# A decoder layer on one core: attention's buffers and bias move into dead memory of the mixers, and the sample's keys are chosen in the mixers' last slots

## The chip, the cores and the metric

The kernel runs on one core of a Trainium2 chip. The metric is the device time in microseconds (us) of one execution. Engines: TensorE (PE) multiplies and transposes, VectorE (DVE) and ScalarE (ACT) do the elementwise work, GpSimd (POOL) and SyncE (SP) issue most of the DMAs. Each engine runs its own instructions in order; they meet at semaphores only.

## The reference

One inference step of one decoder layer: 1024 prompt tokens and 64 sample tokens (8 sequences of 8), model width 1024. Two parts of it bear on the change. A lightweight indexer scores every key for every query and each query keeps its 256 best admissible keys; attention then runs over those alone, with a learned bias by distance. The chunk recurrence of the retention heads is the other mixer, computed beside the projections.

```
u = rmsnorm(x);  z = u @ w_in -> qa, ka, va (attention), qi, ki, wi (indexer), qr, kr, vr, gr (retention)
score[t,s] = sum_h wi[t,h] * relu(qi[t,h] . ki[s]) * 64**-0.5        # s > t excluded
idx = top_k(score, 256)
logits = (qa . ka[idx]) * 64**-0.5 + rel_bias[bucket(pos - idx)]     # 8 heads of 64
att = softmax(logits) @ va[idx]
h = x + concat(att, silu(gr) * groupnorm(retention)) @ w_out
out = h + moe(rmsnorm(h))                                            # top-1 of 4 groups, top-2 of 8 experts
```

For a sample query the keys are 2048 past ones, read from a paged cache, and the 8 new ones of its sequence. In the kernel the sample's scores are one tile `sc_s` of 64 queries by 2112 keys (2048 past and 64 new).

## The kernel before, in words

The kernel is one program with stages one after the other, each a function with a block of code for each engine. A stage ends when all engines are through with its block; then the stage's semaphores are cleared (`stage_semaphores`), with a barrier over all engines. Tokens are worked on in 9 tiles: 8 of 128 prompt tokens and one (number 8) of 64 sample tokens. The stages that matter here, in order:

- `gate` computes the retention gate. It also makes the bias rows and writes a skewed copy of them to DRAM (`skew`), from which one load for each head gives the bias of a whole row of query blocks. The semaphore `skewed` counts these writes.
- `index_scores` writes the scores: `sc` holds those of prompt blocks 2 to 7, one behind the other, 4224 columns of f32; `sc_s` those of the sample.
- `mixers` is a list of 54 projections (units), three for each tile in two rounds, with one slot of code for each unit on each engine. In the first round (units 0 to 26) they are the retention's q, k and v, in the second (27 to 53) attention's q, k and v. The weights of column group c lie in `w[:, c]`, and PE reads the normalised tokens from `uT`. Each projection is 8 matmuls (each shown as two in the trace). In the same slots a bisection halves the bounds of every query's threshold 32 times; ACT counts for the sample and two blocks, DVE for the others. Its last step falls into unit 40. From unit 41 on, `choose` makes one prompt block's mask in each slot (6 blocks, units 41 to 46): keys above the upper bound are in, and of those between the bounds as many, in order, as are still missing. Nothing of this kind stands in slots 47 to 54. In the second round DVE also sums squares and scales the heads of q and k (L758 to L769), and POOL stores K and V (L427, L429).
- `prompt_attention` goes through 32 units: block 7 down to block 0, four pairs of heads each. For each unit PE computes the scores (L1115) and adds the mask (L1121); DVE adds the bias and takes the row's maximum for each head (L1236), ACT exponentiates (L1176), DVE scales (L1245), PE transposes (L1137), ACT copies (L1187), PE multiplies with the values (L1150), and DVE copies out (L1202). PE may overwrite a unit's scores only after both of DVE's passes of the unit before. SP loads the bias of the 8 heads at the start of this stage (L1103). On DVE one step of `choose_for_sample` stands behind each second unit from unit 8 to unit 20: seven steps on the 64 by 2112 scores, which give `mask_s`. Its last large step writes `mask_s` in another order of keys than it reads (by `rearrange`), as `sample_attention` wants them.
- `sample_attention`, the output projection, the router, the experts and the combination follow.

The buffers of prompt attention (logits, probabilities and their transposes, the bias) have memory of their own, taken after that of the mixers is given back. Which slot a step falls into is written out by hand in the unit loops.

Of the kernel before, what the change touches and what calls it, by code (L numbers as in the profile page):

```python
# [6 lines left out]
ALU = mybir.AluOpType  # L7
ACT = mybir.ActivationFunctionType
F32 = mybir.dt.float32
BF16 = mybir.dt.bfloat16  # L10
# [323 lines left out]

def mixers(nc, S, A, X):

# [19 lines left out]
    with ExitStack() as ctx:  # L356
# [43 lines left out]
        def _(sp):  # L400
# [14 lines left out]
            for half in range(2):  # L415
                sp.dma_start(S["ret_prompt"].rearrange("(pr hh) d e -> hh d pr e", hh=2)[half],
                             state[half * HD:(half + 1) * HD, :, :]).then_inc(state_stored, 16)
            sp.wait_ge(s0_stored, 16 * 2 * DB)
            sp.wait_ge(state_stored, 32)
# [235 lines left out]
        def _(dve):  # L655
# [116 lines left out]
            def choose(i):  # L772
                s = X["sc"](i)
                n = s.shape[1]
                above, band, place = junk[:, :n], junk[:, SEQ:SEQ + n], A["va"][:, 6:8, :].rearrange("p i w -> p (i w)")[:, :n]
                link(nc.vector.tensor_scalar(above, s, X["hi"][:, i:i + 1], None, ALU.is_gt, ALU.add, accum_out=found[:, i:i + 1]))
                link(nc.vector.scalar_tensor_tensor(band, s, X["lo"][:, i:i + 1], above, ALU.is_ge, ALU.subtract))
                link(nc.vector.tensor_scalar(left[:, i:i + 1], found[:, i:i + 1], -1.0, float(TOPK), ALU.mult, ALU.add))
                link(nc.vector.tensor_tensor_scan(place, band, band, 0.0, ALU.add, ALU.max))
                link(nc.vector.scalar_tensor_tensor(band, place, left[:, i:i + 1], band, ALU.is_le, ALU.mult))  # L780
                link(nc.vector.scalar_tensor_tensor(X["mask"](i), band, -1.0, above, ALU.add, ALU.add))

            for u in range(UNITS + 1):
                p, c = divmod(u, 3)
# [40 lines left out]
                if 0 <= u - CHOOSE < len(blocks):  # L825
                    choose(blocks[u - CHOOSE])


# [235 lines left out]

def prompt_attention(nc, S, A, X, T, skewed):

# [7 lines left out]
    with ExitStack() as ctx:  # L1074
        sb = lambda n, s, d=F32: ctx.enter_context(nc.sbuf_tensor("a_" + n, s, d))
        sem = stage_semaphores(nc, ctx, "a_")
        logit = sb("logit", [P, 2, SEQ])
        prob = sb("prob", [P, 2, 2, SEQ])
        probT = sb("probT", [P, 2, 2, NT, P])
        peak = sb("peak", [P, 2])  # L1080
# [9 lines left out]
        block = ctx.enter_context(nc.Block())  # L1090
        bias_loaded = [sem(f"bias{pr}_loaded") for pr in range(PAIRS)]
        above, band, place = sb("above", [NS, NK], BF16), sb("band", [NS, NK], BF16), sb("place", [NS, NK])
        found, want, dve_done = sb("found", [NS, 1]), sb("want", [NS, 1]), sem("dve_done")
        half = lambda hh: slice(hh * HD, hh * HD + HD)
        keys = A["kaF"][:, :NT * W].rearrange("p (i a t) -> p i a t", i=NT, a=PAIRS)

        @block.sync
        def _(sp):
            sp.wait_ge(skewed, 16 * 2 * H)
            for h in range(H):  # L1100
                src = S["skew"][h].rearrange("p l -> (p l)")
                src = src[P - 1:P - 1 + P * (SEQ + P - 1)].rearrange("(p l) -> p l", l=SEQ + P - 1)[:, :SEQ]
                sp.dma_start(T["bias"][:, h, :], src).then_inc(bias_loaded[h // 2], 16)  # L1103

# [93 lines left out]
        def _(dve):  # L1198
# [4 lines left out]

            link = Chain(dve, dve_done)

            def choose_for_sample(step):
                s, lo, hi = X["sc_s"][:, :], X["lo"][:NS, NT:], X["hi"][:NS, NT:]
                if step == 0:
                    link(nc.vector.tensor_scalar(above[:, :], s, hi, None, ALU.is_gt, ALU.add, accum_out=found[:, :]))
                elif step == 1:  # L1210
                    link(nc.vector.tensor_scalar(want[:, :], found[:, :], -1.0, float(TOPK), ALU.mult, ALU.add))
                    link(nc.vector.scalar_tensor_tensor(band[:, :], s, lo, above[:, :], ALU.is_ge, ALU.subtract))
                elif step == 2:
                    link(nc.vector.tensor_tensor_scan(place[:, :PAST // 2], band[:, :PAST // 2], band[:, :PAST // 2], 0.0, ALU.add, ALU.max))
                elif step == 3:
                    link(nc.vector.tensor_tensor_scan(place[:, PAST // 2:], band[:, PAST // 2:], band[:, PAST // 2:],
                                                      place[:, PAST // 2 - 1:PAST // 2], ALU.add, ALU.max))
                elif step == 4:
                    link(nc.vector.scalar_tensor_tensor(band[:, :], place[:, :], want[:, :], band[:, :], ALU.is_le, ALU.mult))
                elif step == 5:  # L1220
                    link(nc.vector.scalar_tensor_tensor(X["mask_s"][:, :PAST].rearrange("q (r k) -> q k r", r=16),
                                                        band[:, :PAST].rearrange("q (k r) -> q k r", r=16), -1.0,
                                                        above[:, :PAST].rearrange("q (k r) -> q k r", r=16), ALU.add, ALU.add))
                elif step == 6:
                    link(nc.vector.scalar_tensor_tensor(X["mask_s"][:, PAST:], band[:, PAST:], -1.0, above[:, PAST:], ALU.add, ALU.add))

            for u, (i, pr) in enumerate(units):
                n, off = (i + 1) * P, SEQ - (i + 1) * P
                if u < PAIRS:
                    dve.wait_ge(bias_loaded[pr], 32)  # L1230
                for hh in range(2):
# [15 lines left out]
                if u >= 2:  # L1247
                    take_out(u - 2)
                if u >= 8 and u % 2 == 0:
                    choose_for_sample((u - 8) // 2)  # L1250
            take_out(len(units) - 2)
# [950 lines left out]
def build(nc, a, outs, c):  # L2202
# [20 lines left out]
    with ExitStack() as top:  # L2223
# [29 lines left out]
        with ExitStack() as early:  # L2253
# [8 lines left out]
            total = at[NT - 1] + NT * P  # L2262
            skewed = stage_semaphores(nc, early, "bias_")("skewed")
            sc = sb(early, "sc", [P, total])
            X["sc"] = lambda i: sc[:, at[i]:at[i] + (i + 1) * P]
            X["mask"] = lambda i: X["sc"](i).bitcast(BF16)[:, :(i + 1) * P]
            X["sc_s"] = sb(early, "sc_s", [NS, NK])
            X["lo"], X["hi"] = sb(early, "lo", [P, TILES]), sb(early, "hi", [P, TILES])

            with ExitStack() as st:  # L2270
# [39 lines left out]
                A["w"] = sb(st, "w", [P, 3, KD, W])  # L2310
                gate(nc, S, A, w_gate, gate_loaded, sc[:, :D], skewed)
                A["qiT"] = va_flat[:, :2 * TOK].rearrange("p (a t) -> p a t", a=2)
# [4 lines left out]
                index_scores(nc, S, A, X)  # L2317
                mixers(nc, S, A, X)
            with ExitStack() as st:
                T["bias"] = sb(st, "bias", [P, H, SEQ])  # L2320
                prompt_attention(nc, S, A, X, T, skewed)
            load_constants(nc, "l4_", [], [(A["qaT_s"], A["att"](NT), 1.0, 0.0), (A["kaT_s"], A["ka"](NT), 1.0, 0.0),
# [40 lines left out]
```

## Time and profile before

| | us |
|---|---|
| median of 3 runs | 1778.38 |
| lowest, highest | 1778.3, 1784.95 |
| the profiled execution's own time | 1778.77 |
| its span, first to last instruction | 1776.8 |
| mean granted clock of PE, share of full speed | 0.912 |

Busy times in the span: PE 1502.7 us, DVE 752.2, ACT 510.4, POOL 170.0. The profile is one execution. A view by stretch gives the busy time of each engine between two moments; the timeline shows instructions in order of time, alike ones merged, with the idle time before them and what ended it; a wait names the instruction that came last. PEclk is the clock that PE was granted, 1.00 for 2.4 GHz and 0.50 for 1.2 GHz. PEld is PE's weight load, which runs beside its matmuls. SPq and POOLq are queues of DMA issues.

### The profile page before, as it was taken

Reading aid. Unit: us, or ns where it says so; the run is one execution under the profiler, and the core shown is the slowest. Engines: PE = TensorE matmul, PEld = TensorE weight load, DVE = VectorE, ACT = ScalarE, POOL = GpSimd, SP = SyncE. Lnnn points to the kernel's source line nnn. Section 1 sums busy time; section 2 is a strip of 40 time slices with the busy share of each in tenths; the row PEclk is TensorE's granted clock in tenths of the full one; section 3 lists DMA queues with packets and bytes.
Section 4 is the critical chain, followed back from the end, with each engine's and each line's share of the span. In section 5 each row is a group of like instructions: output and inputs, shape, how many; then the busy total and the mean of one; then the engine's idle time right before and its main releaser. Section 6 shows DMA issues by size and latency. Waiting matters only on the chain. (4 is left out here: it accounts for less than half of the span.)

```text
span 1776.8 us, 20243 instructions
## 1 busy us (share of the span) xinstructions
PE 1502.7 (85%) x7317; PEld 776.1 (44%) x7331; DVE 752.2 (42%) x1900; ACT 510.4 (29%) x958; POOL 170.0 (10%) x226
## 2 busy tenths in 40 slices
PE   3999879999999999798758988899609999999940
PEld 2455324545544444365425655455304444444430
DVE  4002625587778785378834554122331111111105
ACT  3112422535457731365513332000001111111100
POOL 0001000000000000000032330000041000010005
PEclk7899659899999999899879999899859999999975
DMA  7722220001040000200078994683117999999738
GB/s 207 213 105 100 75 78 17 1 1 25 1 142 22 24 24 24 107 1 1 1 251 361 373 379 165 228 303 117 36 19 242 352 354 354 351 355 353 255 103 304
DMA packets 152647, 285.36 MB, mean 161 GB/s; under 512 B 36776, under 2 KB 106056, under 8 KB 144200
## 3 DMA queue, kind: packets, MB, share of 16 engines
q1 hardware_dynamic: 127600, 164.35, 28.2%
q0 software_dynamic: 21264, 106.88, 16.4%
q10 hardware_dynamic: 3696, 12.98, 1.9%
q8 instruction: 53, 0.87, 0.2%
q14 instruction: 34, 0.28, 0.0%
HBM read 243.04 MB, written 46.26 MB: 163 GB/s over the span
## 5 line engine op out<-in xcount | busy, mean ns | idle before, releaser
L443 PE MATMUL x_psZ<-w,uT 128*128 128x512 f32 (+1 forms) x864 | 385.0, 601 | 6.3 <-PEq L64 6.3
L443 PEld LDWEIGHTS x_psZ<-w,uT 128*128 128x128 f32 (+1 forms) x864 | 157.2, 186 | 205.1 <-issue 204.1
L1907 PE MATMUL e_psG<-e_wgu,e_xT 128*96 128x512 f32 x512 | 227.5, 597 | 1.4 <-DVE e_xT L1962 1.4
L1973 DVE TENSOR_TENSOR e_h<-e_gate,e_psG 96x256 f32<-96x256 f32 x32 | 13.4, 418 | 311.3 <-ACT e_gate L1940 311.3
L1907 PEld LDWEIGHTS e_psG<-e_wgu,e_xT 128*96 128x96 f32 x512 | 81.6, 164 | 122.7 <-issue 122.7
L1557 PE MATMUL o_ps<-o_w,k_mixT 128*128 128x512 f32 (+1 forms) x288 | 129.4, 604 | 6.2 <-DMA o_w<-in_w_out 6.2
L1895 PE MATMUL e_psY<-e_wd,e_hT 128*96 128x512 f32 x256 | 115.2, 593 | 1.7 <-ACT e_hT L1946 1.7
L1040 DVE TENSOR_SCALAR_CACHE_REDUCE x_junk<-sc,x_mid 128x384 bf16<-128x384 f32 (+3 forms) x128 | 109.2, 909 | 1.1
L1329 PE MATMUL s_psK<-k_identity,s_ring 128*128 128x128 f32 x512 | 78.5, 297 | 33.9 <-DMA s_ring<-in_cache_k,k_quarter_id 14.2
L1329 PEld LDWEIGHTS s_psK<-k_identity,s_ring 128*128 128x128 f32 x512 | 58.7, 149 | 63.5 <-issue 23.2
L1557 PEld LDWEIGHTS o_ps<-o_w,k_mixT 128*128 128x128 f32 (+1 forms) x288 | 52.6, 188 | 71.0 <-issue 63.4
L1432 DVE COPY s_kcT<-s_psK 128x512 f32<-128x512 f32 x64 | 44.2, 691 | 68.1 <-PE s_psK L1329 68.1
L1023 ACT ACTIVATE mask_s<-sc_s,x_nmid 64x2112 bf16<-64x2112 f32 x32 | 65.7, 2052 | 21.9 <-DVE x_nmid L1036 21.9
L1115 PE MATMUL a_psS<-kaF,k_mixT 64*128 64x512 f32 (+3 forms) x192 | 43.5, 561 | 28.5 <-DVE a_peak L1236 23.8
L1930 ACT ACTIVATE e_y<-e_psY 96x1024 f32<-96x1024 f32 x32 | 32.6, 1019 | 119.5 <-PE e_psY L1895 119.5
L1405 ACT ACTIVATE s_kcT<-s_psK 128x512 f32<-128x512 f32 x64 | 38.1, 595 | 95.7 <-PE s_psK L1329 95.7
L244 PE MATMUL gt_ps<-uT,va 128*128 128x512 f32 (+1 forms) x192 | 65.0, 502 | 0.0
L1882 PE MATMUL e_psX<-k_identity,e_xg 96*128 96x96 f32 x256 | 27.1, 250 | 42.6 <-DMA e_xg<-xn_rows,e_ids 42.6
L1895 PEld LDWEIGHTS e_psY<-e_wd,e_hT 128*96 128x96 f32 x256 | 39.3, 163 | 53.6 <-issue 51.7
L1940 ACT ACTIVATE e_gate<-e_psG 96x256 f32<-96x256 f32 x32 | 12.1, 379 | 174.3 <-PE e_psG L1907 174.3
L1023 ACT ACTIVATE mask_s<-sc,x_nmid 128x1024 bf16<-128x1024 f32 x64 | 59.8, 935 | 2.1
L1176 ACT ACTIVATE a_prob<-a_logit,a_neg 128x1024 f32<-128x1024 f32 (+7 forms) x64 | 49.4, 772 | 36.1 <-DVE a_neg L1239 36.0
(334 smaller groups left out, 1999.5 us busy)
## 6 DMA issues: line engine op xcount, KB each, us to landing
e_wgu<-in_w_gate SPq DMA_DIRECT2D x32, 1024.0 KB, 10.0
e_wgu<-in_w_up SPq DMA_DIRECT2D x32, 1024.0 KB, 13.0
e_wd<-in_w_down SPq DMA_DIRECT2D x32, 1024.0 KB, 7.7
w<-in_w_in SPq DMA_DIRECT2D x6, 2048.0 KB, 9.0
y_rows<-e_y ACTq DMA_DIRECT2D x32, 384.0 KB, 7.2
y_rows<-sc SPq DMA_DIRECT2D x16, 512.0 KB, 15.7
skew<-bias_rows SPq DMA_DIRECT2D x8, 576.0 KB
n_x<-in_x_prompt SPq DMA_DIRECT2D x8, 512.0 KB, 4.2
```

The costliest lines, as they stand in the source:

```text
L244: mm = nc.tensor.matmul(ps[q % 2][:, :width(t)], w[:, k, b * P:(b + 1) * P], A["uT"][:, k, t * P:t * P + width(t)], start=(k == 0), stop=( ...
L443: mm = nc.tensor.matmul(psZ[u % 2][:rows_of(i), :], A["uT"][:, k, cols_of(i)], w[:, c, k, :], start=(k == 0), stop=(k == KD - 1))
L1023: nc.scalar.activation(junk_act[:n, :view(i).shape[1]], view(i), ACT.Sign, bias=nmid[:n, i:i + 1], accum_out=count[:n, i:i + 1]).then_inc( ...
L1040: nc.vector.tensor_scalar(junk[:, junk_at[j]:junk_at[j + 1]], view(i), mid[:, i:i + 1], None, ALU.is_ge, ALU.add, accum_out=count[:, i:i + ...
L1115: nc.tensor.matmul(psS[hh][:, k0:k0 + n].rearrange("p (i t) -> p i t", t=P), A["att"](i)[half(hh), pr, :], keys[half(hh), k0 // P:(k0 + n) ...
L1176: nc.scalar.activation(prob[:, u % 2, hh, :n], logit[:, hh, :n], ACT.Exp, bias=neg[:, hh:hh + 1], accum_out=total[:, u % 2, hh:hh + 1]).th ...
L1329: mm = nc.tensor.transpose(psK[:, q % 2, r * P:(r + 1) * P], ring[:, slot, r, pair(pr)], A["identity"][:, :])
L1405: nc.scalar.activation(kcT[:, c % 2, pr, :], psK[:, 0, :], ACT.Copy).then_inc(k_taken[0], 1)
L1432: nc.vector.tensor_copy(kcT[:, c % 2, pr, :], psK[:, 1, :]).then_inc(k_taken[1], 1)
L1557: mm = nc.tensor.matmul(ps[:n, i % 2, half * 512:(half + 1) * 512], A["mix"](i)[:, k, :], w[:, k, half * 512:(half + 1) * 512], start=(k = ...
L1895: mm = nc.tensor.matmul(psY[:, b, c * 512:(c + 1) * 512], hT[:, b, f, :], wd[:, j % RING, f, c * 512:(c + 1) * 512], start=(f == 0), stop= ...
L1907: mm = nc.tensor.matmul(psG[:CAP, b, :], xT[:, b, k, :], wgu[:, j, k, :], start=(k == 0), stop=(k == KD - 1))
```

## The change

Attention's three large buffers become views on memory that the mixers no longer need: logits and probabilities on `uT`, transposed probabilities on `w[:, 2]`, the bias on `w[:, 0:2]`. With the bias living there, its eight loads are issued by SP in the mixers: those of heads 0 to 3 when the last projection that reads `w[:, 0]` is done, those of heads 4 to 7 when the last that reads `w[:, 1]` is. Their semaphores are now taken at the start of the layer. As there is no memory to give back between the mixers and attention, the semaphores of that scope (`early_`) are released after attention and not before it.

`choose_for_sample` moves from attention's loop to the mixers' slots 47 to 52, one step each. It has six steps, since the two pieces of the mask stand together. The band is written over the scores in f32 (it was a bf16 tile), the running count goes to the upper half of `sc`, and the last piece writes `mask_s` in the order of memory and reads its two inputs across it. For that the prompt masks are packed in the lower half of `sc`.

```diff
@@ def mixers(nc, S, A, X, T), at the end of sync
+            sp.wait_ge(T["skewed"], 16 * 2 * H)
+            for h in range(H):
+                if h % 4 == 0:
+                    sp.wait_ge(z_ready, UNITS - 2 + h // 4)
+                src = S["skew"][h].rearrange("p l -> (p l)")
+                src = src[P - 1:P - 1 + P * (SEQ + P - 1)].rearrange("(p l) -> p l", l=SEQ + P - 1)[:, :SEQ]
+                sp.dma_start(T["bias"][:, h, :], src).then_inc(T["bias_loaded"][h // 2], 16)
             sp.wait_ge(s0_stored, 16 * 2 * DB)
             sp.wait_ge(state_stored, 32)
@@ mixers, vector
+            def choose_for_sample(step):
+                s, lo, hi, c = X["sc_s"][:, :], X["lo"][:NS, NT:], X["hi"][:NS, NT:], slice(NT, NT + 1)
+                above, place = junk[:NS, :NK], X["sc_spare"][:NS, :]
+                by_row = lambda a: a[:, :PAST].rearrange("q (k r) -> q r k", r=16)
+                half = NK // 2
+                if step == 0:
+                    link(nc.vector.tensor_scalar(above, s, hi, None, ALU.is_gt, ALU.add, accum_out=found[:NS, c]))
+                elif step == 1:
+                    link(nc.vector.tensor_scalar(left[:NS, c], found[:NS, c], -1.0, float(TOPK), ALU.mult, ALU.add))
+                    link(nc.vector.scalar_tensor_tensor(s, s, lo, above, ALU.is_ge, ALU.subtract))
+                elif step == 2:
+                    link(nc.vector.tensor_tensor_scan(place[:, :half], s[:, :half], s[:, :half], 0.0, ALU.add, ALU.max))
+                elif step == 3:
+                    link(nc.vector.tensor_tensor_scan(place[:, half:], s[:, half:], s[:, half:], place[:, half - 1:half], ALU.add, ALU.max))
+                elif step == 4:
+                    link(nc.vector.scalar_tensor_tensor(s, place, left[:NS, c], s, ALU.is_le, ALU.mult))
+                elif step == 5:
+                    link(nc.vector.scalar_tensor_tensor(X["mask_s"][:, PAST:], s[:, PAST:], -1.0, above[:, PAST:], ALU.add, ALU.add))
+                    link(nc.vector.scalar_tensor_tensor(X["mask_s"][:, :PAST].rearrange("q (r k) -> q r k", r=16), by_row(s), -1.0,
+                                                        by_row(above), ALU.add, ALU.add))
@@ mixers, vector, in the loop over slots, behind choose
+                if 0 <= u - CHOOSE - len(blocks):
+                    choose_for_sample(u - CHOOSE - len(blocks))
@@ def prompt_attention
-        logit = sb("logit", [P, 2, SEQ])
-        prob = sb("prob", [P, 2, 2, SEQ])
-        probT = sb("probT", [P, 2, 2, NT, P])
+        spare = A["uT"][:, :, :].rearrange("p k t -> p (k t)")
+        logit = spare[:, :2 * SEQ].rearrange("p (a s) -> p a s", a=2)
+        prob = spare[:, 2 * SEQ:6 * SEQ].rearrange("p (j a s) -> p j a s", j=2, a=2)
+        probT = A["w"][:, 2, :, :].rearrange("p k n -> p (k n)").rearrange("p (j a b t) -> p j a b t", j=2, a=2, b=NT)
-        @block.sync
-        def _(sp):
-            sp.wait_ge(skewed, 16 * 2 * H)
...
-                if u >= 8 and u % 2 == 0:
-                    choose_for_sample((u - 8) // 2)
@@ def build
-            X["mask"] = lambda i: X["sc"](i).bitcast(BF16)[:, :(i + 1) * P]
+            X["mask"] = lambda i: sc[:, :].bitcast(BF16)[:, at[i]:at[i] + (i + 1) * P]
+            X["sc_spare"] = sc[:, total - NK:]
...
+                T["bias"] = A["w"][:, 0:2, :, :].rearrange("p c k n -> p (c k n)").rearrange("p (h s) -> p h s", h=H)
...
-            with ExitStack() as st:
-                T["bias"] = sb(st, "bias", [P, H, SEQ])
-                prompt_attention(nc, S, A, X, T, skewed)
+                prompt_attention(nc, A, X, T)
```

## Rows read from the trace of the kernel before

**Rows 1.** Busy time by stretch; (x) counts instructions, PEclk is the granted clock.

```profile
core 0: us, PE busy (x) PEld busy (x) DVE busy (x) ACT busy (x) POOL busy (x), PEclk, DMA share, GB/s
...
679.00:722.00 43.00, 42.82 (x112) 19.54 (x110) 13.45 (x24) 8.55 (x20) 2.69 (x5) 1.00 0.08 31
...
722.00:728.00 6.00, 0.88 (x6) 0.70 (x8) 0.00 (x0) 1.48 (x4) 0.54 (x1) 0.94 0.11 44
...
790.00:862.00 72.00, 53.98 (x475) 35.28 (x480) 61.48 (x139) 35.63 (x86) 0.00 (x0) 0.93 0.01 1
```

**Rows 2.** Timeline over the seam: start, duration, engine, line, operation, [idle before <-releaser].

```profile
707.49 13.90 PE L443 MATMUL x_psZ<-w,uT 128*128 128x512 f32 x32
...
722.31 0.54 POOL L429 DMA_DIRECT2D out<-va  x1 [2.98 <-ACT va L570]
...
727.71 5.45 SPq L1103 DMA_DIRECT2D bias<-skew  x8
...
731.34 0.81 PE L1121 MATMUL a_psS<-sc,k_identity_b 128*128 128x512 bf16 x3 [0.16 <-issue]
...
734.86 1.22 DVE L1236 CUSTOM_DVE_ANT_0 a_logit<-a_psS,bias 128x1024 f32<-128x1024 f32 x1 [16.36 <-DMA bias<-skew]
...
737.48 3.69 PE L1115 MATMUL a_psS<-kaF,k_mixT 64*128 64x512 f32 x8 [5.33 <-DVE a_peak L1236]
...
744.51 1.99 PE L1115 MATMUL a_psS<-kaF,k_mixT 64*128 64x512 f32 x8
```

**Rows 3.** Groups by line, attention: shapes, count, busy us, mean ns, idle before.

```profile
L1221 DVE SCALAR_TENSOR_TENSOR mask_s<-a_band,a_above 64x2048 bf16<-64x2048 bf16 x1 | 9.3, 9253 | 0.0
...
L1216 DVE TENSOR_TENSOR_SCAN a_place<-a_band,a_place 64x1088 f32<-64x1088 bf16 x1 | 2.5, 2467 | 0.0
...
L1212 DVE SCALAR_TENSOR_TENSOR a_band<-sc_s,lo,a_above 64x2112 bf16<-64x2112 f32 x1 | 2.4, 2410 | 0.0
...
L1219 DVE SCALAR_TENSOR_TENSOR a_band<-a_place,a_want,a_band 64x2112 bf16<-64x2112 f32 x1 | 2.4, 2400 | 0.0
...
L1209 DVE TENSOR_SCALAR_CACHE_REDUCE a_above<-sc_s,hi 64x2112 bf16<-64x2112 f32 x1 | 2.4, 2394 | 0.0
...
L1214 DVE TENSOR_TENSOR_SCAN a_place<-a_band 64x1024 f32<-64x1024 bf16 x1 | 2.3, 2273 | 0.0
...
L1225 DVE SCALAR_TENSOR_TENSOR mask_s<-a_band,a_above 64x64 bf16<-64x64 bf16 x1 | 0.2, 206 | 0.0
```

**Rows 4.** Waits of PE, 794 to 858 us: in total, times, longest.

```profile
PE a_psS L1115 <- DVE a_peak L1236: 17.0, 6, 9.1
```

**Rows 5.** Timeline of PE in attention, around the longest step.

```profile
844.28 1.13 PE L1115 MATMUL a_psS<-kaF,k_mixT 64*128 64x512 f32 x4
...
847.49 0.66 PE L1150 MATMUL a_psO<-a_probT,va 128*64 128x128 f32 x8
...
857.27 1.65 PE L1115 MATMUL a_psS<-kaF,k_mixT 64*128 64x384 f32 x4 [9.12 <-DVE a_peak L1236]
...
862.23 0.92 PE L1115 MATMUL a_psS<-kaF,k_mixT 64*128 64x384 f32 x4
```

**Rows 6.** Busy time by stretch, around the longest step.

```profile
845.00:857.00 12.00, 2.99 (x27) 1.86 (x26) 11.40 (x9) 1.55 (x4) 0.00 (x0) 0.72 0.00 0
```

**Rows 7.** Timeline: the last K store is issued.

```profile
718.79 0.54 POOL L427 DMA_DIRECT2D out<-x_nat  x1 [17.42 <-DVE x_nat L769]
```

**Rows 8.** DVE, single lines: duration min/median/max in ns, first and last start.

```profile
L1466 DVE COPY s_bias<-s_logit x1: 2401/2401/2401, 916.8 to 916.8; 128x2048 f32<-128x2048 f32 x1
...
L1751 DVE TENSOR_REDUCE g_el<-g_prod x1: 660/660/660, 1280.8 to 1280.8; 128x72 f32<-128x288 f32 x1
...
L1784 DVE TENSOR_REDUCE g_s<-g_prod x6: 452/453/455, 1292.2 to 1298.3; 128x9 f32<-128x288 f32 x6
```

**Rows 9.** DMA issues by line: count, KB each, median us to landing.

```profile
bias<-skew SPq DMA_DIRECT2D x8, 512.0 KB, 8.3
out<-va POOLq DMA_DIRECT2D x4, 256.0 KB, 2.5
```

More of the change, by code:

```diff
@@ L332, in _, with mixers @@
             pool.wait_ge(stored[1], 16 * (TILES // 2))
-def mixers(nc, S, A, X):
+def mixers(nc, S, A, X, T):
     order = [NT] + list(range(NT))
@@ L1058, in bisection, with prompt_attention @@
     return act_step, dve_begin, count_keys, move_bounds, junk
-def prompt_attention(nc, S, A, X, T, skewed):
+def prompt_attention(nc, A, X, T):
     units = [(i, pr) for i in reversed(range(NT)) for pr in range(PAIRS)]
@@ L1090, in prompt_attention @@
         block = ctx.enter_context(nc.Block())
-        bias_loaded = [sem(f"bias{pr}_loaded") for pr in range(PAIRS)]
-        above, band, place = sb("above", [NS, NK], BF16), sb("band", [NS, NK], BF16), sb("place", [NS, NK])
-        found, want, dve_done = sb("found", [NS, 1]), sb("want", [NS, 1]), sem("dve_done")
         half = lambda hh: slice(hh * HD, hh * HD + HD)
         keys = A["kaF"][:, :NT * W].rearrange("p (i a t) -> p i a t", i=NT, a=PAIRS)
-        @block.sync
-        def _(sp):
-            sp.wait_ge(skewed, 16 * 2 * H)
[L1100 to L1103, printed above, removed]
         @block.tensor
@@ L1202, in take_out @@
                 nc.vector.tensor_copy(A["att"](i)[:, pr, :], psO[:, u % 2, :P]).then_inc(o_taken, 1)
[L1204 to L1225, printed above, removed]
             for u, (i, pr) in enumerate(units):
@@ L1229, in _ @@
                 if u < PAIRS:
-                    dve.wait_ge(bias_loaded[pr], 32)
+                    dve.wait_ge(T["bias_loaded"][pr], 32)
                 for hh in range(2):
@@ L2262, in build @@
             total = at[NT - 1] + NT * P
-            skewed = stage_semaphores(nc, early, "bias_")("skewed")
+            of_bias = stage_semaphores(nc, early, "bias_")
+            T["skewed"], T["bias_loaded"] = of_bias("skewed"), [of_bias(f"loaded{pr}") for pr in range(PAIRS)]
             sc = sb(early, "sc", [P, total])
             X["sc"] = lambda i: sc[:, at[i]:at[i] + (i + 1) * P]
-            X["mask"] = lambda i: X["sc"](i).bitcast(BF16)[:, :(i + 1) * P]
+            X["mask"] = lambda i: sc[:, :].bitcast(BF16)[:, at[i]:at[i] + (i + 1) * P]
+            X["sc_spare"] = sc[:, total - NK:]
             X["sc_s"] = sb(early, "sc_s", [NS, NK])
@@ L2310, in build @@
                 A["w"] = sb(st, "w", [P, 3, KD, W])
-                gate(nc, S, A, w_gate, gate_loaded, sc[:, :D], skewed)
+                T["bias"] = A["w"][:, 0:2, :, :].rearrange("p c k n -> p (c k n)").rearrange("p (h s) -> p h s", h=H)
+                gate(nc, S, A, w_gate, gate_loaded, sc[:, :D], T["skewed"])
                 A["qiT"] = va_flat[:, :2 * TOK].rearrange("p (a t) -> p a t", a=2)
@@ L2317, in build @@
                 index_scores(nc, S, A, X)
-                mixers(nc, S, A, X)
-            with ExitStack() as st:
-                T["bias"] = sb(st, "bias", [P, H, SEQ])
-                prompt_attention(nc, S, A, X, T, skewed)
+                mixers(nc, S, A, X, T)
+                prompt_attention(nc, A, X, T)
             load_constants(nc, "l4_", [], [(A["qaT_s"], A["att"](NT), 1.0, 0.0), (A["kaT_s"], A["ka"](NT), 1.0, 0.0),
```

## The prediction

> **What bounds the kernel now.** I read the busy times by stretch first, since the change touches three stages and nothing else [rows 1]. At the end of the mixers (679 to 722 us) PE is busy 42.8 of 43 us at full clock and VectorE (DVE) 13.45 of 43: PE is the bound, DVE has some 29 us of room. In attention's blocks 5 to 3 (790 to 862 us) it is the other way round: PE 54.0 of 72 us, DVE 61.5. Between the two lies a seam, 722 to 728 us, in which PE has 0.9 us of work. Second, the timeline over the seam [rows 2]: the last V store is issued at 722.31, attention begins at 727.7 with eight loads of the bias, the scores of the first unit are there at 732.15 (731.34 and 0.81), but DVE adds the bias only at 734.86 and PE comes back at 737.48. Third, the groups of DVE's choose steps in attention [rows 3], and what PE waited for from 794 to 858 us: 17.0 us in 6 waits, each before the next scores, for DVE's peak [rows 4].
>
> **1. The seven choose steps leave attention (gain).** They cost 2.39, 2.41, 2.27, 2.47, 2.40, 9.25 and 0.21 us [rows 3], with a read-out and a small scalar 21.6 us of DVE time. DVE runs in order, so each sits in front of the next unit's two logit passes; PE, which needs those to free psS, waits. That is the 17.0 us in 6 waits, the longest 9.12 before 857.27 [rows 4, 5]. It is less than 21.6, since PE is a little behind DVE in units without a step and takes up part of each. With the steps gone, is DVE late next? No: of its 61.5 us [rows 1] 21.4 are these steps; 40.1 remain for what PE does in 54 us. PE becomes the bound, so the whole 17.0 us goes. There is a second part. In the long wait the granted clock falls (mean 0.72 over 845 to 857 us [rows 6]), and PE starts slow at 857.27: its next turn of scores, transposes and values lasts until 862.23, 4.96 us [rows 5]. The same round before it, begun at 844.28 with the larger scores of block 3, had its last values issued at 847.5 and ended by 848.15, 3.8 to 3.9 us; the score matmuls show the size, 1.65 us at 857.27 against 0.92 at 862.23 [rows 5]. Less 0.2 us for the smaller scores that round would take 3.6, so I take 1.4 us (bounds 0.7, from the score matmuls alone, and 1.6). Sum of part 1: 17.0 + 1.4 = 18.4 us.
>
> **2. The bias is read before the mixers end (gain).** SyncE now issues the loads of heads 0 to 3 when the last tile's first projection is done, and of heads 4 to 7 one projection later. PE does the last two projections from 707.49 to 721.4, with 0.6 us of transposes ahead of them [rows 2], so a projection is 7.0 us and the two moments are 707 and 714.4. Before, eight issues took 5.45 us of the queue and a load landed 8.3 us after its issue [rows 2, 9]; half of them would be in by 707 + 2.7 + 8.3 = 718, the others by 725.5 at that pace, and half the traffic at a time lands sooner. Attention starts at 727.7 and its first unit needs heads 0 and 1 only, so the wait is gone. What is late next is PE's first mask matmul: the logit pass can start at about 732.0 (the first head's mask is a little before 732.15) and not at 734.86. Gain 2.9 us (bounds 0 and 2.9 for the wait alone). PE then starts the second scores at 734.6 and not 737.48. Whether it starts slow, as before (3.69 us against 1.99 at 744.51 [rows 2]), is open: the idle stretch is 2.5 us and no longer 5.3. I take the same slow start; a clock that holds would give 1.7 us more.
> What is queued behind the moved loads: on SyncE only its waits for the stores of the states, issued some twenty projections earlier. The other queue is POOL's, with the last K and V stores. K is issued at 718.79, V at 722.31 and lands 2.5 us later at 724.8 [rows 2, 7, 9]; this landing ends the mixers. The second half of the bias (2.1 MB) starts at 714.4 and shares the DMA engines with the K store. The V store meets at most its tail. I take 0, bounds 0 and 2.5 us (a landing twice as long).
>
> **3. The choose steps enter the last slots of the mixers.** One step in each of slots 47 to 52: 2.5, 2.5, 2.35, 2.35, 2.4 and the last. The scans are 1056 long, between 2.27 for 1024 and 2.47 for 1088 [rows 3]; the band is f32 now, the same element count. Slots are some 7 us and DVE works 13.45 of 43 us in them [rows 1], so 14.6 us more fit, and what stands behind a step on DVE (scaling of heads, K's gain) is wanted by PE only a slot later. Cover gone would cost the step, 2.4 us each. The exception is the last, in slot 52: on DVE it stands between the last sum of squares and the scaling whose result is the K store at 718.79 [rows 7] and PE's last transpose. POOL issues in order, K and then V, 0.54 us an issue, V at 722.31. So K may be issued as late as 721.77: DVE can lose 2.98 us there. The last step is a 64-wide piece (0.21) and the 2048-wide one, which I call T: the cost to the end of the mixers is T - 2.75, if that is positive.
> T is not in the trace. It was 9.25 us for bf16 inputs in order and a bf16 output scattered at 256 bytes [rows 3]. Now the output is in order and both inputs are scattered (f32 at 64 bytes, bf16 at 32). Nearest rows: two inputs and all in order, 2.40 for 2112 [rows 3]; an f32 output scattered at 512 bytes, 2.40 for 2048 [rows 8]; an f32 input in steps of 32 bytes, 288 elements, 660 ns against 453 in order [rows 8], 0.72 ns more an element, which is 1.5 us on 2048 for one input and 3.0 for two. So T lies between 2.35 and 9.25, with 5.3 between them. The nearest rows say that what was dear was the 2-byte scattered write, since a 4-byte one was not. I take T = 2.4, cost 0; bounds 0 and 6.5 us.
> This last part is where a rule speaks against the change. The trace first: the scattered f32 write took 1.17 ns an element, the scattered bf16 write 4.5 [rows 3, 8]. The Trainium skill, "SBUF — State Buffer", section "Door 1: The DMA port swizzle", has a note by which accesses are only free while at least two of them hit the same 16-byte line; both new inputs go to another line with every element. By that rule T would stay near 9 us, the sum 6.5 us less; by the rows on f32 it would be 2.4. The f32 write at 512 bytes does not agree with the rule, the f32 read [rows 8] agrees in part.
>
> **4. Buffers.** Logits, probabilities and their transposes lie in memory that the mixers are done with; same shapes, same instructions: 0. One release of semaphores moves from before attention to behind it; both places are on the path: 0, bounds -0.5 and +0.5. Masks lie elsewhere, with the same width: 0.
>
> **Sum.** 18.4 + 2.9 = 21.3 us. The profiled execution took 1778.77 us (span 1776.8 and 2.0 around it), which makes 1757.5. It stands 0.4 above the median of the runs shown, 1778.38, so against that 1757.1. All later stages begin behind barriers and shift as one.
>
> **Rivals.**
> A. The scattered reads are as dear as the scattered write. For it: the steps of 64 and 32 bytes, and the reduction with a scattered input [rows 8]. Against: the f32 row at 512 bytes. The mixers end 6.5 us later: gain 14.8, 1763.6 us. Chance 0.15.
> B. The bias traffic holds up the last stores, or comes in no earlier than before. For it: at 8.3 us a load the last ones would land at 725.5, behind the V store. Against: only 2.1 MB are under way after 714.4. Price up to 2.5 us, or the 2.9 of part 2: about 1760. Chance 0.10.
> C. Slower than before: T by itself is so long that it eats everything. That begins where T - 2.75 is over 21.3, T over 24 us or 11.8 ns an element, 2.6 times the dearest DVE row here (4.5 ns). At 14 ns, T is 29 us and the time 1783. For it speaks only that two inputs are scattered and not one output. Chance 0.03. Milder, T of 15 to 24 us, would leave it within the band of no change: 0.03.
> D. The change does not do what it says in attention: DVE's own order of work holds PE up after all, with no step in it. DVE has 40.1 us of work for PE's 54.0 [rows 1], so it could be so only in single units where two passes and two scalings come late together; at 0.2 to 0.3 us in each of ten units it costs 2 or 3 of the 17.0 us: 1760. Chance 0.06.
>
> **How the numbers follow.** The forecast has 0.63, the rest as above (A 0.15, B 0.10, D 0.06, C 0.03, and 0.03 for its milder form). A measurement of this kernel tells about 0.5%, 8.9 us, from no change: forecast, A, B and D are all beyond it, 0.94 faster, 0.03 within, 0.03 slower. Range: from 1753 (a clock that holds 1.7, part 1 with 19.5, the release) to 1764 (A whole, B and D on their own).
>
> **What would show it.** Right: no DVE op on sc_s after 728; PE waits for the peak of under 2 us in all from 785 to 850; first logit pass some 4.3 us after attention's first matmul (7.1 now); PE at 99% to the end of the mixers; V store issued about 722.3. Wrong: the last step over 3 us and V's issue later by T - 2.75; a landing of V over 3 us; DVE waits that appear in front of each logit pass; an attention stage that is shorter by less than 19 us.

## The result, and the profile after

The changed kernel takes 1756.3 us (median of 4 runs, 1752.1 to 1757.49) for 1778.89 before (4 runs); the ratio is 0.987, 95% interval 0.984 to 0.989. In a later set of runs it was 1756.97 (4 runs) for 1776.56 (7 runs), ratio 0.989 (0.988 to 0.991). Forecast were 1757, 1753 to 1764. Single runs of one kernel spread over 4 to 12 us, so parts of 1 or 2 us are read from the profile's stages and not from medians.

The profiled execution took 1752.1 us, span 1750.3, which is 26.5 less than before. Not all of that is the change's. The last tile's transposes of Q begin at 715.06, before at 721.22, and PE was already some 6 us ahead around 500 us, where no line had changed; its mean granted clock over the first 400 us was 0.88 and before 0.85. So the stages are measured from their own first instruction:

| stage, from one profile each | before | after |
|---|---|---|
| last tile's Q transposes to attention's first matmul | 6.53 us | 7.25 |
| from there to DVE's first logit pass | 7.11 | 4.92 |
| attention, first matmul to the end of the last copy-out | 167.1 | 146.4 |
| from there to the next stage's first DVE operation | 0.81 | 1.20 |

Busy times by stretch of the changed kernel, same columns as [rows 1]:

```profile
core 0: us, PE busy (x) PEld busy (x) DVE busy (x) ACT busy (x) POOL busy (x), PEclk, DMA share, GB/s
...
679.00:722.00 43.00, 37.29 (x102) 17.27 (x100) 23.16 (x27) 9.10 (x19) 2.59 (x5) 0.98 0.37 135
...
722.00:728.00 6.00, 4.99 (x11) 1.71 (x12) 0.77 (x1) 1.28 (x1) 0.00 (x0) 0.57 0.00 0
...
790.00:850.00 60.00, 59.20 (x527) 37.78 (x530) 46.41 (x165) 40.52 (x104) 0.00 (x0) 1.00 0.01 1
```

In attention (790 to 850) PE is busy 59.2 of 60 us, where it was 54.0 of 72 [rows 1], and DVE, with 46.4 of 60, has less work than PE. The mixers' end now holds 23 us of DVE work. PE's waits for DVE's peak over the whole stage of attention, in total, times and longest, before and after:

```profile
PE a_psS L1115 <- DVE a_peak L1236: 23.8, 12, 9.1
```

```profile
PE a_psS L1135 <- DVE a_peak L1233: 3.7, 6, 2.2
```

Of the 20.1 us between the two, 17.0 are the six waits of [rows 4], all gone. The other 3.1 us are the wait before the second unit's scores, 5.33 us [rows 2] and now 2.21.

The choose steps in the mixers, groups by line (busy us and mean ns). Five cost what they cost in attention [rows 3] to within 0.07 us, though the band is f32; the large last one, L808, takes 3.92 us for 9.25:

```profile
L808 DVE SCALAR_TENSOR_TENSOR mask_s<-sc_s,x_junk 64x2048 bf16<-64x2048 f32 x1 | 3.9, 3921 | 0.0
...
L799 DVE SCALAR_TENSOR_TENSOR sc_s<-sc_s,lo,x_junk 64x2112 f32<-64x2112 f32 x1 | 2.4, 2410 | 0.0
...
L805 DVE SCALAR_TENSOR_TENSOR sc_s<-sc,x_left,sc_s 64x2112 f32<-64x2112 f32 x1 | 2.4, 2403 | 0.0
...
L803 DVE TENSOR_TENSOR_SCAN sc<-sc_s,sc 64x1056 f32<-64x1056 f32 x1 | 2.4, 2402 | 0.0
...
L796 DVE TENSOR_SCALAR_CACHE_REDUCE x_junk<-sc_s,hi 64x2112 bf16<-64x2112 f32 x1 | 2.4, 2397 | 0.0
...
L801 DVE TENSOR_TENSOR_SCAN sc<-sc_s 64x1056 f32<-64x1056 f32 x1 | 2.3, 2342 | 0.0
```

And the timeline over the seam, to be laid beside [rows 2, 7]:

```profile
710.56 3.92 DVE L808 SCALAR_TENSOR_TENSOR mask_s<-sc_s,x_junk 64x2048 bf16<-64x2048 f32 x1
...
716.46 0.54 POOL L434 DMA_DIRECT2D out<-x_nat  x1 [21.25 <-DVE x_nat L776]
...
716.99 0.54 POOL L436 DMA_DIRECT2D out<-va  x1
...
722.31 3.78 PE L1135 MATMUL a_psS<-kaF,k_mixT 64*128 64x512 f32 x8 [5.11 <-PEq L64]
...
726.43 1.21 PE L1141 MATMUL a_psS<-sc,k_identity_b 128*128 128x512 bf16 x3 [0.34 <-issue]
...
727.23 1.23 DVE L1233 CUSTOM_DVE_ANT_0 uT<-a_psS,w 128x1024 f32<-128x1024 f32 x1 [11.06 <-PE a_psS L1141]
...
729.84 3.04 PE L1135 MATMUL a_psS<-kaF,k_mixT 64*128 64x512 f32 x8 [2.21 <-DVE a_peak L1233]
```

The last step runs until 714.5, so K's scaling ends at 716.2 and the K store is issued at 716.46, 1.4 us behind the transposes of Q; it was 2.4 us ahead of them. POOL issues V right behind, at 716.99. The clock is at its lower level when attention begins (0.57 over 722 to 728), so the masks end only at 727.6, and the logit pass waits for them and no more for the bias.

### The profile page after: what moved, and what is told of

Its sections match the earlier page's. It is cut to its first block and busy times, and to the rows that moved or that the text cites. A ratio compares the mean times of both kernels' runs of the same rounds, so it can differ in the third digit from the quotient of the medians.

```text
span 1750.3 us, 20250 instructions
## 1 busy us (share of the span) xinstructions
PE 1496.6 (86%) x7317; PEld 772.8 (44%) x7331; DVE 746.7 (43%) x1900; ACT 509.8 (29%) x958; POOL 169.3 (10%) x226
## 5 line engine op out<-in xcount | busy, mean ns | idle before, releaser
L1324 PE MATMUL s_psK<-k_identity,s_ring 128*128 128x128 f32 x512 | 80.0, 302 | 34.4 <-DMA s_ring<-in_cache_k,k_quarter_id 14.8
L1207 ACT ACTIVATE w<-a_psT 128x512 f32<-128x512 f32 (+3 forms) x96 | 43.3, 486 | 42.6 <-PE a_psT L1157 42.4
L1596 ACT ACTIVATE o_xn<-o_h 128x1024 f32<-128x1024 f32 (+1 forms) x9 | 9.5, 1057 | 154.7 <-DVE o_h L1618 154.7
```

The source lines that it names most:

```text
L1207: nc.scalar.activation(probT[:, u % 2, hh, b0:b0 + nb, :], psT[:, t % 2, :nb, :], ACT.Copy).then_inc(t_taken, 1)
L1324: mm = nc.tensor.transpose(psK[:, q % 2, r * P:(r + 1) * P], ring[:, slot, r, pair(pr)], A["identity"][:, :])
```

## The experiments

**Only the bias goes back.** The edit to the changed kernel:

```diff
@@ mixers, sync
-            sp.wait_ge(T["skewed"], 16 * 2 * H)
-            for h in range(H):
-                if h % 4 == 0:
-                    sp.wait_ge(z_ready, UNITS - 2 + h // 4)
...
@@ prompt_attention
+        @block.sync
+        def _(sp):
+            sp.wait_ge(T["skewed"], 16 * 2 * H)
+            for h in range(H):
...
+                sp.dma_start(T["bias"][:, h, :], src).then_inc(T["bias_loaded"][h // 2], 16)
```

> The changed kernel, but the eight loads of the bias are issued at the start of attention again (into the same memory); the choose steps stay in the mixers. My theory: the early bias is worth what DVE's first logit pass comes sooner. In the changed kernel it started 4.9 us after attention's first matmul, before 7.15, so attention grows from 146.4 to about 148.6 us (at most 149.3, the 2.9 us of the prediction) and the time from 1756.3 to 1758.5. Rival 1: the wait also cools PE's clock, and the second scores start slower: 150 us or more, 1760. Rival 2: the early bias is worth nothing, since the first masks end late at half clock: attention stays at 146.4 to 147.

Measured: 1758.26 us (1753.93 to 1759.5), ratio to before 0.989 (0.987 to 0.991), which is the changed kernel's. Attention took 144.9 us and the first logit pass came 4.97 us after the first matmul, with the bias 4.92. The timeline of this kernel:

```profile
728.88 3.79 PE L1136 MATMUL a_psS<-kaF,k_mixT 64*128 64x512 f32 x8 [5.08 <-PEq L64]
...
733.00 1.49 PE L1142 MATMUL a_psS<-sc,k_identity_b 128*128 128x512 bf16 x3 [0.33 <-issue]
...
733.85 1.22 DVE L1234 CUSTOM_DVE_ANT_0 uT<-a_psS,w 128x1024 f32<-128x1024 f32 x1 [11.10 <-DMA w<-skew]
...
736.46 1.99 PE L1136 MATMUL a_psS<-kaF,k_mixT 64*128 64x512 f32 x8 [1.97 <-DVE a_peak L1234]
```

DVE starts at 733.85, on a bias that has just landed, 0.85 us after PE began the masks. In the changed kernel, where the bias had long been there, the pass came 0.80 us after the masks' start (727.23 and 726.43). So rival 2 holds: with the first masks at half clock and the loads at full rate the early bias is worth 0.05 us here. Nor is rival 1 right: this time the clock came back before the second scores (1.99 us), which made attention 1.5 us shorter than the changed kernel's. Why it came back is open. The late loads are not enough to bring it about: in the third and the fourth experiment, which load late too, the second scores took 2.95 and 3.64 us. The start of the stage, first scores to third, shows no gain of the early bias beyond this scatter: 12.9, 14.5 and 14.8 us in the three kernels of the experiments that load it late, 13.7 to 14.5 us in five profiles that load it early. The reason that 7.11 us stood in the first profile is the rate of the loads. Busy time by stretch, the last two columns the share of the DMA engines and GB/s; the kernel before, then the same lines at the same distance from attention's start in the kernel of the third experiment, which loads the bias in the same way:

```profile
730.00:731.00 1.00, 1.00 (x4) 0.00 (x0) 0.00 (x0) 0.00 (x0) 0.00 (x0) 0.65 0.72 254
...
732.00:733.00 1.00, 0.15 (x1) 0.00 (x0) 0.00 (x0) 0.00 (x0) 0.00 (x0) 1.00 0.86 279
```

```profile
725.00:726.00 1.00, 1.00 (x4) 0.00 (x0) 0.00 (x0) 0.00 (x0) 0.00 (x0) 0.50 1.01 385
...
727.00:728.00 1.00, 1.00 (x3) 0.15 (x1) 0.05 (x1) 0.00 (x0) 0.00 (x0) 0.50 0.97 377
```

In the three microseconds from the first of these lines on it is 250 to 280 GB/s against 352 to 385; the two other kernels that load late, of the first and the fourth experiment, had 377 to 422 there. So the loads were slow in the one execution from which the 2.9 us were read; why is open.

**Only the choose steps go back.** The edit moves the seven steps and their text from the kernel before into attention's loop; the running count stays in the spare half of `sc`, for want of room:

```diff
@@ mixers, vector
-                if 0 <= u - CHOOSE - len(blocks):
-                    choose_for_sample(u - CHOOSE - len(blocks))
@@ prompt_attention, vector
+                if u >= 8 and u % 2 == 0:
+                    choose_for_sample((u - 8) // 2)
```

> The changed kernel, but the choose steps stand behind every second unit of attention again, in the old order and with the scattered bf16 write; the bias is loaded early. My theory: PE waits for DVE's peak before the next scores, 17 us in 6 waits, and the clock falls in the long one: attention takes 146.4 + 18.4 = 165 us, the time is 1775 (18.4 more, less about 0.8 us by which the last V store comes sooner). The mixers' last V store is issued 0.9 us after PE's last projection and not 1.75. Rival: much of the step time was hidden by the bias' wait or by PE's own work, and the gain of the change came from the bias and the buffers: attention under 158 us, time under 1768.

Measured: 1774.87 us (1769.71 to 1779.64), ratio to before 0.9988 (0.997 to 1.000); attention 165.1 us. PE's waits in attention:

```profile
PE a_psS L1135 <- DVE a_peak L1256: 21.1, 12, 9.1
```

By its interval this one edit leaves between none and 5 of the some 20 us gained. The steps cost attention 165.1 - 146.4 = 18.7 us, and 18.4 was the prediction's sum for them. The rival (half of it hidden) is out by 7 us.

**The order of the last step alone**, on the kernel before:

```diff
@@ prompt_attention, vector, step 5
-                    link(nc.vector.scalar_tensor_tensor(X["mask_s"][:, :PAST].rearrange("q (r k) -> q k r", r=16),
-                                                        band[:, :PAST].rearrange("q (k r) -> q k r", r=16), -1.0,
-                                                        above[:, :PAST].rearrange("q (k r) -> q k r", r=16), ALU.add, ALU.add))
+                    link(nc.vector.scalar_tensor_tensor(X["mask_s"][:, :PAST].rearrange("q (r k) -> q r k", r=16),
+                                                        band[:, :PAST].rearrange("q (k r) -> q r k", r=16), -1.0,
+                                                        above[:, :PAST].rearrange("q (k r) -> q r k", r=16), ALU.add, ALU.add))
```

> The kernel before with one edit: the large last step reads its two bf16 inputs scattered and writes mask_s in order, instead of the reverse. Everything else as before. My theory: scattered reads cost less than scattered 2-byte writes; in the changed kernel, with one f32 and one bf16 input, the step took 3.92 us for 9.25. With two bf16 inputs I expect 3.9 or less. The longest wait of PE shrinks from 9.1 to 3.8 us or less and the clock holds: 5.3 + 1.4 = 6.7 us, time 1772. Rival: bf16 reads at 32 bytes are as dear as the writes (over 8 us), and in the changed kernel the f32 input made it cheap: no gain, 1779. Rival 2: the clock falls all the same in a wait of 3.8 us: 5.3 us, 1773.6.

Measured: 1771.38 us (1766.7 to 1776.26), ratio 0.9975 (0.996 to 0.999): 5.3 us less than the 1776.63 of the kernel before in the same set of runs, by the interval 2 to 7 us. The step, duration in ns; then PE's score matmuls with their waits; then the clock behind the longest wait:

```profile
L1221 DVE SCALAR_TENSOR_TENSOR mask_s<-a_band,a_above x1: 3861/3861/3861, 840.4 to 840.4; 64x2048 bf16<-64x2048 bf16 x1
```

```profile
822.92 1.44 PE L1115 MATMUL a_psS<-kaF,k_mixT 64*128 64x512 f32 x4 [1.94 <-DVE a_peak L1236]
...
828.74 1.13 PE L1115 MATMUL a_psS<-kaF,k_mixT 64*128 64x512 f32 x4
...
834.49 1.13 PE L1115 MATMUL a_psS<-kaF,k_mixT 64*128 64x512 f32 x4 [1.67 <-DVE a_peak L1236]
...
845.89 1.65 PE L1115 MATMUL a_psS<-kaF,k_mixT 64*128 64x384 f32 x4 [3.73 <-DVE a_peak L1236]
...
851.67 0.92 PE L1115 MATMUL a_psS<-kaF,k_mixT 64*128 64x384 f32 x4
```

```profile
845.00:848.00 3.00, 2.11 (x6) 0.87 (x7) 2.36 (x9) 2.00 (x5) 0.00 (x0) 0.50 0.00 0
...
848.00:850.00 2.00, 2.00 (x13) 1.37 (x11) 1.43 (x7) 0.82 (x2) 0.00 (x0) 0.50 0.00 0
```

The step takes 3.86 us and PE waits 3.73 instead of 9.12 us [rows 5]. But the clock falls in this wait too: the scores after it take 1.65 us and the clock is 0.50 up to 850. The round behind the wait (845.89 to 851.67) takes 5.78 us, where it took 4.96 before [rows 5]. So my theory that the clock holds is wrong, and the second rival is right about the clock; but the wait is shorter by 5.4 us and 0.8 of that goes back in the slower round, which leaves 4.6 us at this place. The whole stage took 162.5 us: 4.6 less than before with its slow loads, 3.4 less than in the fourth experiment. There the clock held in a wait of 1.95 us like the one before 822.92; here it fell in that wait (scores 1.44 us for 1.13), and the 5.82 us to the next scores are 1.6 us more than the 4.23 before. So about a quarter of what the change gains (4.6 of 19.6 us by the stages, 5.3 by the medians) can be had by turning one `rearrange`.

**Only the buffers.** Both edits above that put something back, together.

> Of the change only the buffers: attention's large buffers and the bias in the mixers' dead memory, the release of one scope's semaphores behind attention; the bias is loaded at attention's start and the choose steps stand in attention as before. My theory: 0 us, time 1778.9 within 2, attention 167 us, first logit pass 7.1 us after the first matmul. Rival: other addresses or the moved release matter by more than 2 us in either direction (then the stage from the last V store to attention's first matmul, 5.4 us, or the durations of L1236, L1176 and L1187 differ).

Measured: 1774.45 us (1770.85 to 1783.07), ratio 0.999 (0.997 to 1.001). Attention takes 165.9 us. The timeline at its start:

```profile
723.53 3.79 PE L1136 MATMUL a_psS<-kaF,k_mixT 64*128 64x512 f32 x8 [3.97 <-PEq L64]
...
728.41 1.22 DVE L1257 CUSTOM_DVE_ANT_0 uT<-a_psS,w 128x1024 f32<-128x1024 f32 x1 [13.72 <-DMA w<-skew]
```

The first logit pass comes 4.88 us after the first matmul, where the expectation had 7.1 from the profile before: again the rate of the bias. The time differs from the kernel before by no more than the noise. The release of semaphores that moved shows as 0.4 us less ahead of attention (6.12 us from the Q transposes, before 6.53) and 0.4 more behind it (1.21 for 0.81).

**What makes the scattered step dear.** Nine added operations, out = (a - 1) + b. The text on record has them in every slot; they stand once, behind the last slot, and write dead memory only. With 38 us of added work on DVE the one run took 1794.84 us; only the durations count.

```diff
+            op = lambda o, a, b: link(nc.vector.scalar_tensor_tensor(o, a, -1.0, b, ALU.add, ALU.add))
+            op(flat(b_out), flat(f_in), flat(b_in))
+            op(flat(b_out), by16(f_in), flat(b_in))
...
+            op(by128(f_out), flat(f_in), flat(b_in))
```

> The changed kernel with nine added operations on DVE in every slot of the mixers, each out = (a - 1) + b over 64 x 2048, on memory that is overwritten or dead; the added passes overwrite scores and masks, so only the durations count, not the result or the time. In order: (1) all in order, f32 and bf16 in, bf16 out; (2) f32 input at 64 bytes; (3) bf16 input at 32 bytes; (4) two bf16 inputs, one at 32 bytes; (5) f32 input at 512 bytes; (6) bf16 output at 32 bytes; (7) bf16 output at 256 bytes; (8) f32 output at 64 bytes; (9) f32 output at 512 bytes. Known so far: both inputs scattered (64 and 32 bytes) 3.92 us, two bf16 inputs scattered 3.86, bf16 output at 256 bytes 9.25. My theory: the dear thing is a scattered write of 2 bytes: (6) and (7) about 9, (8) and (9) about 2.4, (1) 2.35, and a scattered input costs about 0.8 us each, (2), (3) and (4) 3.1. Rival, by 16-byte lines: whatever touches another line with each element pays alike, in or out, so (2), (3), (5), (8) and (9) would be equal, near 3.9, and the 9.25 of (7) is left unexplained. Second rival: what costs in (7) is the distance of 256 bytes, not the write of 2 bytes: (6) is then near 3.9.

The timeline of DVE (start, duration), operations 1 to 8 in order; the ninth took 3.6 us:

```profile
719.32 2.28 DVE L863 SCALAR_TENSOR_TENSOR sc<-sc_s,x_junk 64x2048 bf16<-64x2048 f32 x1
...
721.63 3.58 DVE L863 SCALAR_TENSOR_TENSOR sc<-sc_s,x_junk 64x2048 bf16<-64x2048 f32 x1
...
725.24 3.82 DVE L863 SCALAR_TENSOR_TENSOR sc<-sc_s,x_junk 64x2048 bf16<-64x2048 f32 x1
...
729.10 3.81 DVE L863 SCALAR_TENSOR_TENSOR sc<-x_junk 64x2048 bf16<-64x2048 bf16 x1
...
732.95 3.61 DVE L863 SCALAR_TENSOR_TENSOR sc<-sc_s,x_junk 64x2048 bf16<-64x2048 f32 x1
...
736.59 8.72 DVE L863 SCALAR_TENSOR_TENSOR sc<-sc_s,x_junk 64x2048 bf16<-64x2048 f32 x1
...
745.34 9.25 DVE L863 SCALAR_TENSOR_TENSOR sc<-sc_s,x_junk 64x2048 bf16<-64x2048 f32 x1
...
754.63 3.58 DVE L863 SCALAR_TENSOR_TENSOR sc<-sc_s,x_junk 64x2048 f32<-64x2048 f32 x1
```

| what is scattered, of 64 x 2048 | us | ns an element |
|---|---|---|
| nothing | 2.28 | 1.11 |
| f32 input, 64 or 512 bytes apart | 3.58, 3.61 | 1.75 |
| bf16 input, 32 bytes apart | 3.82, 3.81 | 1.86 |
| f32 output, 64 or 512 bytes apart | 3.58, 3.6 | 1.75 |
| bf16 output, 32 or 256 bytes apart | 8.72, 9.25 | 4.3, 4.5 |

My theory was right about the 2-byte writes (8.72 and 9.25) and wrong about the f32 outputs, which it had at 2.4 and not 3.6. The rival's equality holds: scattering costs 1.3 to 1.5 us wherever it stands, input or output, near or far, and two scattered inputs cost no more than one (3.92 in L808). On top of that a scattered write of 2-byte elements costs 5 us more. The second rival is out: bf16 outputs only 32 bytes apart take 8.72 us, so the distance hardly matters.

**The last step one slot later.**

```diff
-                if 0 <= u - CHOOSE - len(blocks):
-                    choose_for_sample(u - CHOOSE - len(blocks))
+                q = u - CHOOSE - len(blocks)
+                if 0 <= q < 5:
+                    choose_for_sample(q)
+                elif q == 6:
+                    choose_for_sample(5)
```

> The changed kernel with the last choose step one slot later, behind the scaling of the last tile's K heads. My theory: the step (3.92 us) held back the last K store, and POOL issues V only behind K, so V came 0.84 us late and so did attention. With the step one slot later K and V are issued as before the change, V 0.9 us after PE's last projection, and attention starts 0.8 us sooner; the step itself ends before PE's last transposes. Rival: the end of the mixers hangs on something else (the bias traffic, PE's last transposes), and attention's first matmul stays 5.3 us plus 1.75 behind the last projection. In the median 0.8 us of 1756 can't be told; the profile's seam decides.

Its base, the changed kernel once more:

> The changed kernel once more, as the base for the next two on the same chip. 1756 us within 2; attention 145 to 146.5 us; last V store issued 1.75 us after PE's last projection.

Measured: base 1756.97 us, attention 146.0, 7.22 us from the Q transposes to attention's first matmul. With the later step 1754.49 us (1751.99 to 1759.75), attention 145.6, and:

```profile
716.53 3.93 DVE L808 SCALAR_TENSOR_TENSOR mask_s<-sc_s,x_junk 64x2048 bf16<-64x2048 f32 x1
...
719.09 0.60 PE L472 MATMUL x_psT<-k_identity,x_nat 128*128 128x128 f32 x4
...
720.18 0.54 POOL L436 DMA_DIRECT2D out<-va  x1 [2.98 <-ACT va L577]
...
725.26 3.49 PE L1138 MATMUL a_psS<-kaF,k_mixT 64*128 64x512 f32 x8 [4.02 <-PEq L64]
```

V is issued 1.1 us after the start of the Q transposes, as before the change, and attention begins 6.17 us after it: 1.05 us sooner than in the base. Of this 0.84 us is V's earlier issue (1.93 us after the transposes' start in the base); the other 0.2 lies between V's issue and attention's first matmul, 5.08 us for 5.30. The medians agree in sign, but their ranges overlap.

**The stores' wait moved into attention**, beside it; the tile that K is stored from lives on for it:

```diff
@@ mixers, gpsimd
-            pool.wait_ge(k_stored, 16 * TILES)
-            pool.wait_ge(v_stored, 16 * TILES)
@@ prompt_attention
+        @block.gpsimd
+        def _(pool):
+            pool.wait_ge(T["k_stored"], 16 * TILES)
+            pool.wait_ge(T["v_stored"], 16 * TILES)
```

> The kernel with the last step in the later slot, and the mixers no longer wait for their last K and V stores: that wait is POOL's in attention, and the tile that K is stored from lives on. My theory: the seam (5.3 us from the V store's issue to attention's first matmul) is 2.6 us of the store's landing and the rest release and barrier; without the landing the last to end is ACT's copy of the transposed K, 1.7 us after V's issue and so 0.9 us before the landing; attention starts about 1 us sooner than with the step in the later slot alone. 1754.5 us for 1756.3, at the edge of what can be told. Rival: the landing takes longer than the median says because the bias and K share the engines (over 3.5 us); then it gives 2 us or more. Second rival: the landing is not what the seam waits for: no gain.

Measured: 1755.01 us (1750.33 to 1757.65), ratio to before 0.9886 (0.987 to 0.990).

```profile
716.69 0.60 PE L470 MATMUL x_psT<-k_identity,nat 128*128 128x128 f32 x4
...
717.78 0.54 POOL L436 DMA_DIRECT2D out<-va  x1 [2.98 <-ACT va L575]
...
721.80 3.56 PE L1141 MATMUL a_psS<-kaF,k_mixT 64*128 64x512 f32 x8 [2.97 <-PEq L64]
```

5.11 us from the Q transposes to the first matmul, 1.06 less again, as the theory had it. By the stages this is the fastest version, 2.1 us under the changed kernel; by the medians (1757.0, 1754.5, 1755.0) the three can't be told apart.

## Why the prediction was right, step by step

1. *Choose steps leave attention, 18.4 us.* Right in mechanism and size: 18.7 us from the second experiment, 20.9 between the two kernels that load the bias late (165.9 and 144.9). Of these 20.9, 1.6 arise before the third unit's scores, where the clock of the start differs. From the third scores on the stage takes 150.4 to 151.4 us in the three profiles with steps in the old form and 131.5 to 132.1 in five without: 18.3 to 19.9 us. All of the 17.0 us of waits went, and PE became the bound, as argued from DVE's 40 us. The 1.4 us for the clock behind the long wait was a fair price: the round that took 4.96 us takes 3.47 in the changed kernel. The third experiment shows that it did not hang on the full 9.1 us: the clock falls as well in a wait of 3.7 us.
2. *Early bias, 2.9 us.* Wrong in size: 0.05 us against its experiment, 0.6 between the two kernels with steps in attention (4.88 and 4.31 us to the first logit pass). The step that failed is "the logit pass can start at about 732.0". It took from one profile both a wait for slow loads (250 to 280 GB/s) and masks at a clock that had come back (done 4.4 us after the first matmul, 5.3 in the profile after). With the loads at full rate the truth is 0 to 0.6 us, at the stated bound of 0 or little above it; against that one slow execution it is 2.2 us (7.11 and 4.92).
3. *The last step, T = 2.4 us, cost 0.* T was 3.92. The chain through the last K store was the right one, and T - 2.75 gives 1.17 us: V's issue came 0.84 us later and attention 1.05. What failed is the choice among the rows: "a 4-byte one was not" dear. The f32 write of [rows 8] belongs to a copy with one input, and it was laid beside the 2.40 us of an operation with two inputs. The trace before had copies in order of f32:

```profile
L322 DVE COPY w<-w 128x320 f32<-128x320 f32 x8 | 2.6, 326 | 111.0 <-ACT w L309 111.0
...
L323 DVE COPY w<-w 128x64 f32<-128x64 f32 x8 | 1.5, 186 | 0.0
```

That is 140 ns for 256 more elements, 0.55 ns each, where the scattered copy took 1.17. So 2048 elements in order would take some 1.3 us (an estimate from these two rows) and the scattered write had cost about 1.1 us of its 2.40. The strided reduction beside it had said 1.5 us more, too. The Trainium skill, "SBUF — State Buffer", section "Door 1: The DMA port swizzle", says that an access which goes to another 16-byte line each time pays. The measured 3.6 to 3.8 us for every such form with f32 or bf16 inputs or an f32 output, 2.28 in order, agree with it. The 9 us that the prediction made of it did not come.
4. *Bias traffic against the last stores, 0.* Right. With and without it (the changed kernel and the first experiment) the seam is 7.25 and 7.22 us. The traffic does slow a store that it meets: where K's is issued 2.4 us ahead of the Q transposes and the bias is still coming in (the kernel with the steps back and the one with the later step), it took 5.0 us to land, for 2.3 in the kernel before. But V's lands last.
5. *Buffers and release, 0 within 0.5.* Right: 0.4 less ahead, 0.4 more behind.

The sum by the runs: 18.7 to 20.9 for the steps, 0 to 0.6 for the bias, less 1.05 for the last step, which makes 18 to 20 us. The same stages of the two profiles, from the Q transposes to the next stage's first DVE operation, differ by 19.6 us (174.5 and 154.9), and some 2 of these are the slow loads of the one execution. The second pair of medians gave 19.6, by its interval 16 to 22, the first 22.6. So the mechanism of the largest term was right, while the closeness of 21.3 is in part luck: the bias was too large by 2 to 3 us and the last step's cost missing by 1, and noise of this size can't tell 18 from 21. Of the rivals, B's price of 2.9 us came, but not by its mechanism: the bias did come in early, and the masks ended last. A did not hold (T under 4, not 9), C was far off, and D did not show: PE waited 3.7 us in the whole stage.

## What to carry to other kernels

Work of an engine that runs in order costs most of its time where that engine stands between two steps of another (17.0 us of waits for 21.6 us of steps), and nothing where it has slack. Before sizing it, look for the stage in which the engine idles, and for the one slot there in which something is queued behind it. A wait for a DMA at the seam of two stages should not be priced from one profile: see first what the engine would do without it, at the lower clock too. And before moving a strided operation, turn its access pattern so that the 2-byte side is in order; that alone was worth about a quarter of the gain here.

## What the runs showed of the hardware

- DVE, two inputs, 2048 elements: 2.28 us in order, 3.6 to 3.9 with any f32 operand or bf16 input scattered over 32 bytes or more, 8.7 to 9.3 with a bf16 output scattered. Two scattered inputs cost as much as one.
- PE's granted clock was at 0.50 after waits of 9.1 us and of 3.7 us in attention, but held in the wait before 834.49 of the third experiment (1.67 us, scores at 1.13 us as in undisturbed units). In the same place of the stage a wait of 1.94 or 1.95 us was followed by scores of 1.13 us in three profiles and of 1.44 us in the third experiment, with the clock at 0.60 over 823 to 826. So waits of about 2 us can go either way. It makes 1.5 us in attention between kernels with the same work there (146.4 and 144.9), 0.4 between two profiles of the changed kernel; and the last tile's Q transposes began at 715.06 in one profile of the changed kernel and at 718.27 in the other, with mean clocks of 0.88 and 0.90 over the first 400 us, so the clock alone doesn't order even those.
- The same eight loads of 512 KB ran at 250 to 280 GB/s in one execution and at 352 to 422 in three others, between 2 and 5 us after attention's start.
- The last K store, 256 KB, landed in 2.3 us where no bias was being loaded and in 5.0 us beside its loads.
